# A Transformer layer on one core: the Newton steps of its small reciprocal roots move from VectorE to GpSimd

## What is computed

```
h = x @ w_in                                  # split into q, k, v, z, beta, a (delta rule), q, k, v (attention), two gates
o_a = gated_deltanet(...)                     # conv of 4 taps, silu, l2-norm of q and k, delta rule in chunks of 64
o_b = diff_attention(...)                     # two softmaxes per head, p0 - lam * p1, times v, then RMS norm per head
merged = sigmoid(ga) * (o_a @ w_branch_a) + sigmoid(gb) * (o_b @ w_branch_b)
x = layer_norm(ALPHA * x + merged @ w_out)
ffn = (silu(x @ w_gate) * (x @ w_up)) @ w_down
x = layer_norm(ALPHA * x + ffn)

l2_normalize(x) = x * rsqrt(sum(x * x) + 1e-6)
rms_norm(x, w)  = x * rsqrt(mean(x * x) + 1e-6) * w
```

## Time and profile before

| | |
|---|---|
| median of 3 runs | 2053.83 us (2053.8 to 2054.26) |
| the profiled execution's own time | 2053.67 us |
| its span in the profile | 2051.9 us |
| PE busy | 2003.6 us, 98% |
| DVE busy | 1234.3 us, 60% |
| ACT busy | 915.8 us, 45% |
| POOL busy | 0.2 us, 4 instructions |

### The profile page before, as it was taken

The page is one execution under the profiler, slowest core; times in us unless marked ns, Lnnn a source line. Parts: engine busy times, 40 slices in busy tenths (PEclk is TensorE's granted clock), DMA queues, the critical chain, the costliest instruction groups (busy, mean ns, idle before and its releaser), DMA issues.

```text
span 2051.9 us, 32409 instructions
## 1 busy us (share of the span) xinstructions
PE 2003.6 (98%) x11050; PEld 1649.2 (80%) x11050; DVE 1234.3 (60%) x1750; ACT 915.8 (45%) x1194; POOL 0.2 (0%) x4
## 2 busy tenths in 40 slices
PE   9999999999999999999999999799999999999996
PEld 6887888878887878787888887588888888888884
DVE  7768767587646666767655555644554444554455
ACT  5435344353445555555534433444443444443442
POOL 0000000000000000000000000000000000000000
PEclk9999999999999999999999999999999999999998
DMA  7434343343454545454555676365555555555553
GB/s 252 131 128 134 119 144 131 125 143 114 156 190 158 179 159 183 155 176 163 187 191 190 199 241 214 107 190 190 188 187 195 191 192 190 190 190 192 189 192 140
DMA packets 97961, 353.14 MB, mean 172 GB/s; under 512 B 10816, under 2 KB 11072, under 8 KB 97728
## 3 DMA queue, kind: packets, MB, share of 16 engines
q1 hardware_dynamic: 97856, 351.64, 52.2%
HBM read 349.50 MB, written 2.10 MB: 171 GB/s over the span
## 4 chain that ended last, share of the span: by engine, by line
PE 89%; DVE 5%; ACT 2%; issue 2%; DMA 0%; SPq 0%; DVEq 0%; ACTq 0%
PE pg L337 80%; PE B L337 7%; DVE wlo L989 1%; DVE gates L989 1%; ACT whi L708 1%; PE B L610 1%; DVE cT L997 0%; DMA vn<-in_xT 0%; PE B L410 0%; DVE od L989 0%; PE B L565 0%; DVE pr L997 0%; PE B L586 0%; ACT pr L888 0%; ACT L774 0%
## 5 line engine op out<-in xcount | busy, mean ns | idle before, releaser
L989 DVE TENSOR_TENSOR wlo<-raw,whi 128x1024 fp32r<-128x1024 f32 (+1 forms) x650 | 791.3, 1221 | 626.0 <-ACT whi L708 614.2
L708 ACT ACTIVATE whi<-raw 128x1024 fp32r<-128x1024 f32 (+1 forms) x650 | 684.4, 1057 | 702.3 <-PE pg L337 695.2
L337 PE MATMUL pg<-whi,act_x 128*128 128x512 f32 x3008 | 980.0, 397 | 0.0
L337 PEld LDWEIGHTS pg<-whi,act_x 128*128 128x128 f32 x3008 | 565.1, 188 | 122.6 <-issue 5.5
L337 PE MATMUL pg<-wlo,act_x 128*128 128x512 f32 x1504 | 586.7, 390 | 0.0
L337 PE MATMUL pg<-whi,act_a 128*128 128x512 f32 x1664 | 519.6, 391 | 5.5 <-DVE act_a L989 5.5
L337 PEld LDWEIGHTS pg<-whi,act_a 128*128 128x128 f32 x1664 | 313.2, 188 | 71.7 <-DVE act_a L989 7.2
L337 PEld LDWEIGHTS pg<-wlo,act_x 128*128 128x128 f32 x1504 | 283.1, 188 | 54.4 <-issue 1.2
L337 PE MATMUL pg<-wlo,act_a 128*128 128x512 f32 x832 | 324.7, 390 | 0.0
L337 PEld LDWEIGHTS pg<-wlo,act_a 128*128 128x128 f32 x832 | 156.7, 188 | 31.9
L337 PE MATMUL pg<-whi,act_b 128*128 128x512 f32 x512 | 158.8, 390 | 0.0
(11 more groups left out here) (183 smaller groups left out, 983.8 us busy)
## 6 DMA issues: line engine op xcount, KB each, us to landing
raw<-in_weights SPq DMA_DIRECT2D x646, 512.0 KB, 3.8
gates<-in_ln_in SPq DMA_DIRECT2D x4, 512.0 KB, 6.5
gates<-in_ln_in SPq DMA_DIRECT2D x1, 2048.0 KB, 9.6
out<-gates SPq DMA_DIRECT2D x8, 256.0 KB, 2.5
raw<-in_weights SPq DMA_DIRECT2D x4, 256.0 KB, 4.3
cT<-in_xT SPq DMA_DIRECT2D x2, 512.0 KB, 7.1
qT<-in_xrow SPq DMA_DIRECT2D x2, 512.0 KB, 7.1
kT<-in_xrow SPq DMA_DIRECT2D x2, 512.0 KB, 5.2
```

The source lines that it names most:

```text
L337: return nc.tensor.matmul(o, l, r, start=start, stop=stop)
L708: return nc.scalar.activation(o, i, ACT.Copy, scale=scale)
L989: return V.tensor_tensor(o, a, b, op)
```

## The change

The three Newton steps of `rk`, `rs` and the heads' root go to a program of GpSimd's own (`@block.gpsimd`). DVE keeps the seed, now in one operation (the bits times -0.5 plus the constant) instead of two, and hands it over by a semaphore (`dve_ss`, `dve_qs`, `dve_oss`). GpSimd does four operations per Newton step, 12 per root, each one waiting for the one before it, and hands back by `pool_rinv`, `pool_rs`, `pool_oss`. DVE's `oh` moves from slot s0 + 5 to slot s0 + 6. The layer norms keep `rsqrt` on DVE, with the one-operation seed.

```diff
--- before.py
+++ after.py
@@ -37,7 +37,7 @@
 DA_TURN = [(21, 23), (27, 29)]
 DA_TURN_FIRST = [(10, 12), (18, 20)]
 HEAD_SLOTS = [0, 6, 12, 18]
-CONV_LINKS, BUILD_LINKS, SCAN_LINKS, DA_LINKS = 12, 22, 18, 69
+CONV_LINKS, BUILD_LINKS, SCAN_LINKS, DA_LINKS = 12, 10, 7, 25
 OT_SLOTS = (12, 14)
 XP = [(0, 2), (2, 4), (4, 8), (8, 12), (12, 16)]
 HALVED = 2
@@ -133,6 +133,7 @@
         cw = sb("cw", [P, 3, HB, CONV])
         sm = sb("sm", [P, 72])
         dsm = sb("dsm", [P, NDS])
+        half = sb("half", [P, 8])
         lam = sb("lam", [P, 2])
         g_all = sb("g_all", [P, TOK * HEADS])
         pz = sb("pz", [P, 4, TOK * HEADS])
@@ -219,7 +220,7 @@
             pe_z dve_vn pe_so act_s act_o0 pe_ks dve_r pe_o1 dve_o1 pe_qtok act_osq act_sqq
             dve_oh pe_oT act_oT dve_oT
             pe_qkT act_qkT pe_s dve_s1 dve_mx act_exp dve_pd pe_pT act_pT pe_pv act_oss dve_oh2 pe_oT2
-            act_oT2 dve_oT2 dve_m pe_mT act_mT dve_mT conv_chain build_chain scan_chain da_chain""".split()
+            act_oT2 dve_oT2 dve_m pe_mT act_mT dve_mT dve_qs pool_rs dve_ss pool_rinv dve_oss pool_oss pool_chain conv_chain build_chain scan_chain da_chain""".split()
         N = {n: sem(n) for n in once + counted}
 
         class Chain:
@@ -981,6 +982,36 @@
                 normalize(1, cq)
 
 
+        @block.gpsimd
+        def _(pool):
+            G = nc.gpsimd
+            ch = Chain(pool, N["pool_chain"], 1)
+
+            def root(o, x):
+
+                a = half[:, 0:x.shape[1]]
+                for i in range(3):
+                    ch(G.tensor_tensor(a, o, o, ALU.mult))
+                    ch(G.tensor_tensor(a, a, x, ALU.mult))
+                    ch(G.tensor_scalar(a, a, -0.5, 1.5, ALU.mult, ALU.add))
+                    last = G.tensor_tensor(o, a, o, ALU.mult)
+                    if i < 2:
+                        ch(last)
+                return last
+
+            for j in range(NB + 1):
+                if j > 0:
+                    pool.wait_ge(N["dve_qs"], 1 + j)
+                    root(d_("rs"), d_("qs")).then_inc(N["pool_rs"], 1)
+                if j < NB:
+                    pool.wait_ge(N["dve_ss"], 1 + j + 1)
+                    ch(root(d_("rk"), d_("ss")))
+                    G.tensor_tensor(d_("rinv"), d_("rk"), d_("ss"), ALU.mult).then_inc(N["pool_rinv"], 1)
+            for h in range(HEADS):
+                pool.wait_ge(N["dve_oss"], 1 + h + 1)
+                root(sm[:, 48:50], sm[:, 42:44]).then_inc(N["pool_oss"], 1)
+
+
         @block.vector
         def _(dve):
             V = nc.vector
@@ -996,11 +1027,14 @@
             def stt(o, a, s, b, op0, op1):
                 return V.scalar_tensor_tensor(out=o, in0=a, scalar=s, in1=b, op0=op0, op1=op1)
 
+            def seed(o, x):
+
+                return ts(o.bitcast(I32), x.bitcast(I32), -0.5, ALU.mult, float(0x5F3759DF), ALU.add)
+
             def rsqrt(ch, o, x):
 
                 a = sm[:, 64:64 + x.shape[1]]
-                ch(V.tensor_single_scalar(o.bitcast(I32), x.bitcast(I32), 1, ALU.logical_shift_right))
-                ch(ts(o.bitcast(I32), o.bitcast(I32), -1.0, ALU.mult, float(0x5F3759DF), ALU.add))
+                ch(seed(o, x))
                 for _ in range(3):
                     ch(stt(a, o, -0.5, o, ALU.mult, ALU.mult))
                     ch(tt(a, a, x, ALU.mult))
@@ -1121,6 +1155,7 @@
                     ch(ts(d_("ss"), d_("ss"), RMS_EPS, ALU.add))
                     ch(V.reciprocal(d_("e"), d_("ss")))
                     ch(tt(d_("e"), d_("e"), s_("beta"), ALU.mult))
+                    seed(d_("rk"), d_("ss")).then_inc(N["dve_ss"], 1)
                 if s == 14:
                     dve.wait_ge(N["act_decay"], 1 + j + 1)
                     ch(tt(AT[:, :, :], decm[:, :, :], bc(d_("e"), P), ALU.mult))
@@ -1155,14 +1190,13 @@
                             tt(T[0:CH], T[0:CH], B8[3][0:CH], ALU.subtract)
                             tt(TTf[0:CH, :, 0:CH], TT[0:CH], B8[2][0:CH], ALU.subtract)
                             tt(TTf[CH:P, :, CH:P], TT[CH:P], B8[2][CH:P], ALU.subtract).then_inc(N["dve_t"], 1)
-                if s == 19:
-                    rsqrt(ch, d_("rk"), d_("ss"))
-                    ch(tt(d_("rinv"), d_("rk"), d_("ss"), ALU.mult))
                 if s == 25:
                     ch(tt(decm[:, :, :], decm[:, :, :], rep(c("same"), 8), ALU.mult))
                 if s in (20, 22):
                     t = (s - 20) // 2
                     dve.wait_ge(N["pe_v"], 1 + 2 * j + t + 1)
+                    if t == 0:
+                        dve.wait_ge(N["pool_rinv"], 1 + j + 1)
                     tt(vr[:, t], B4[0], bc(d_("rinv")[:, HB * t:HB * (t + 1)], P), ALU.mult).then_inc(N["dve_v"], 1)
                 if s in (28, 29):
                     t = s - 28
@@ -1196,9 +1230,9 @@
                     ch(V.tensor_reduce(d_("qs"), AT[:, :, :], X, ALU.add))
                     ch(ts(d_("qs"), d_("qs"), P * RMS_EPS, ALU.mult, P * RMS_EPS ** 2, ALU.add))
                     ch(stt(d_("qs"), d_("os"), 1.0 / P, d_("qs"), ALU.mult, ALU.add))
-                if s == 7:
-                    rsqrt(ch, d_("rs"), d_("qs"))
+                    seed(d_("rs"), d_("qs")).then_inc(N["dve_qs"], 1)
                 if s == 10:
+                    dve.wait_ge(N["pool_rs"], 1 + j + 1)
                     for t in range(TOK):
                         tt(od[:, t], od[:, t], bc(d_("rs")[:, HB * t:HB * (t + 1)], P), ALU.mult
                            ).then_inc(N["dve_oh"], 1)
@@ -1258,9 +1292,11 @@
                         ins.then_inc(N["dve_pd"], 1)
                     if s == s0 + 5:
                         dve.wait_ge(N["act_oss"], 1 + HB * j + h + 1)
+                        ch(ts(sm[:, 42:44], sm[:, 40:42], 1.0 / P, ALU.mult, RMS_EPS, ALU.add))
+                        seed(sm[:, 48:50], sm[:, 42:44]).then_inc(N["dve_oss"], 1)
+                    if s == s0 + 6:
+                        dve.wait_ge(N["pool_oss"], 1 + HB * j + h + 1)
                         dve.wait_ge(N["pe_oT2"], 1 + HB * j + h)
-                        ch(ts(sm[:, 42:44], sm[:, 40:42], 1.0 / P, ALU.mult, RMS_EPS, ALU.add))
-                        rsqrt(ch, sm[:, 48:50], sm[:, 42:44])
                         ch(tt(oh[:, :, :], B[3][:, 0:SEQ].rearrange("p (t d) -> p t d", t=TOK), bc(sm[:, 48:50], P),
                               ALU.mult))
                         stt(oh[:, :, :], oh[:, :, :], 1.0 - LAMBDA_INIT, rep(par[:, slice(*PARAM["daw"])], TOK),
```

## The result

| | before | changed |
|---|---|---|
| median, us | 2054.02 (8 runs, 2053.58 to 2054.9) | 2060.37 (8 runs, 2056.86 to 2061.15) |
| profiled execution, us | 2053.67 | 2060.26 |
| its span, us | 2051.9 | 2058.2 |

By the medians the changed kernel is slower by 6.3 us, where 16 were forecast. The ratio is 1.0027, with a 95% interval of 1.0016 to 1.0038, or 5.6 us; that is what the means give (2059.7 and 2054.1), which lie closer together than the medians. The direction was right and the time lies in the range, but the size was off by 10 us: two terms of the sum were mis-sized and a third was missing. The changed kernel's eight runs spread over 4.3 us, where the eight of before spread over 1.3 (in larger groups of 20 to 23 runs, those of before spread over 2.4 to 2.7).

The account below looks back on a forecast made before the run. PE, busy 98% of the span, was taken as the bound. Gains of -2.0 us and +18.0 us for the heads made +16.0 us on 2053.83, say 2070 us; forecast's own range 2058 to 2092, 8-in-10 range 2054 to 2105.

Parts of the forecast that it names:

- T: Attention heads: time of the root on GpSimd with handovers and one standstill, forecast as 5.07 us.
- a link at 0.32 us: GpSimd's root: each of 12 chained operations takes 0.32 us, the geometric middle of 0.20 and 0.50.
- The hold of a whole `wlo`: Heads' root: a GpSimd operation beside DVE's wide `wlo` stands still for its whole 1.13 us.
- the heads' term: Attention bodies: later `oh` and scores make PE wait 4.50 us per body, +18.0 us in four.
- the delta rule's -1.6 us: Delta rule: without the small operations `wlo` and the convolution start 0.54 us earlier, in three bodies -1.6 us.
- the gains: Delta rule's three bodies -1.6 us and both layer norms -0.4 us, together -2.0 us.
- So its wait stays as it is in PE's time: Delta rule: ACT's work up to the decay hangs on the convolution, so PE's three 0.8 us waits remain.
- the root was thus free: Attention head 0: DVE's root only filled time in which DVE would have waited for ACT's `whi` anyway.
- a fall of PE's clock: New PE waits: a fall there would prove the forecast wrong; none seen beside waits of 1 us.
- quick or side by side: Rival: GpSimd is quick or works beside `wlo`, T at most 4.23 us, within 0.2% (4.1 us); chance 0.28.
- Faster: Rival: `oh` ahead of the scores costs nothing and T fits, -2.0 us, 2051.8 us; chance 0.04.
- A slow link: Rival: a GpSimd link of 0.50 us, T = 7.23 us, sum 2109 us; slower than forecast had chance 0.18.

Follow-up runs that it names:

- e4: Changed kernel with two Newton steps instead of three for the heads' root, 8 links instead of 12 and less exact; 2050.06 us.
- e7: Changed kernel with DVE's wait for the root, `oh` and scores ahead of `wlo` at slots 6, 12, 18 and 24; 2049.34 us.
- e1: Changed kernel with the heads' root back on DVE at slot s0 + 5, only the delta rule's two roots on GpSimd; 2048.32 us.
- e10: e3 with the delta rule's `rs` root at slot 9 instead of 7, still on DVE; 2052.89 us.
- e5: Changed kernel with two unused 128x384 matmuls on PE at each body's head 1, ahead of its wait for `pr`; 2055.8 us.
- e3: Kernel before with only the one-operation seed, nothing on GpSimd; 2053.4 us.
- e8: Changed kernel with `oh` left in slot s0 + 5, so that DVE stands still for GpSimd's root; 2058.62 us.
- e9: e3 with the next head's scores ahead of the slot's `wlo` at slots 6, 12 and 18, nothing on GpSimd; 2049.84 us.
- e6: e1 with the next head's scores ahead of the slot's `wlo` at slots 6, 12 and 18; 2043.98 us.
- e2: Changed kernel with the delta rule's roots back on DVE, only the heads' root on GpSimd; 2065.23 us.

## Why the prediction was wrong in size

**The mechanism held.** Forecast were a lower wait at the convolution, waits for `oh`, a longer wait for `pr`, one held link in each head, and the scores of head 1 later by T - 3.13 us. T, from the seed's end to the return, is 740.04 - 735.65 = 4.39 us. The formula gives 1.26 us for the scores, and 5.56 - 4.30 = 1.26 were measured; it gives no wait for `oh` at heads 0 to 2, none seen (16 waits had been forecast, and there are four); 0.58 at head 3, and 0.36 to 0.80 were seen; for `pr` 2.25, measured 2.17. Per body it makes 0.58 + 1.26 = 1.84 us, and 101.6 to 101.7 less 99.77 are 1.8 to 1.9. The 0.80 us at the very last head has another cause than the root: `oh` stands there behind a `wlo` that waits until 1002.40 us for ACT's `whi`, and 0.62 us of it stay in e4, whose root is four links shorter.

**The first failed step: a link at 0.32 us, and so T = 5.07.** Measured is 0.28 us (0.20 of work and 0.08 to the next). The hold of a whole `wlo` was rightly taken; it measured 1.02 us, 1.22 less the operation's own 0.20, against the 1.13 of the sum. T was 0.68 us too long, 0.59 of it in the links and 0.11 in the hold. At T = 4.39 the root is back for `oh` in time at heads 0 to 2, so that a body loses the 1.84 us above and not 4.50, and the heads' term is +7.4 us and not +18.0. The middle between "as on DVE" and "as ACT on 256 columns" should have leaned to the lower bound: it was the row with the same operation and the same few columns, and the memset of 0.10 us had already shown that GpSimd starts an operation quickly.

The Trainium skill's page GPSIMD Engine Reference, section Performance versus the Vector engine, gives the factor 1.96 for an elementwise operation with two inputs, measured at N = 2048. This trace differs for so small an operation: 0.20 us on GpSimd (e7: 193 to 197 ns) against 161 ns on DVE is a factor of 1.2. No run here has a wide operation on GpSimd, so the page's own case is neither borne out nor refuted.

**The second failed step: "the second starts at 298.37 right behind them, though its `whi` was ready at 297.80", the delta rule's -1.6 us.** I paired that `wlo` with the `whi` that was nearest in time. It used the one before it, which ended at 294.89, as the changed kernel shows: there two `wlo` run in a row with no wait for ACT. Timeline of ACT before:

```profile
293.83 1.06 ACT L708 ACTIVATE whi<-raw 128x1024 fp32r<-128x1024 f32 x1
```

So not 0.54 us came off DVE's path to the convolution but the whole root, over 2 us, and with it both of PE's waits, for the convolution and for the decay, 2.7 + 2.5 = 5.2 us. With 0.7 us less waiting for `pr` and 0.2 at the layer norm through the one-operation seed, that is about what e1 gains, 6.0 us; the gains were forecast as 2.0. "So its wait stays as it is in PE's time", said of the decay, fell with it: the decay's wait hangs on all that DVE has to do up to it, as e10 shows, where the convolution is in time and the decay still waits 1.05 us. The same pairing error stands in "the root was thus free" for the heads; there it did not change the sum, since the path from the small chain to the scores was counted from its rows.

**The third: no term for the clock.** The text named a fall of PE's clock as what would make it wrong, and judged by the waits of 1 us, which show none. At 2.17 us it does fall, in two of the four bodies of the profiled execution, 1.6 us each, and e5 puts its price at 4.6 us on the median. The trace of before had a warning: "at the full clock in all but the last slices" was read from digits that stand for 90% or more. The long wait of 8.32 us at the first layer norm, which ends at 1289.10 us, has PE at half its clock from about 1286 to 1296 us (granted clock in a window, before):

```profile
1286.00:1296.00 10.00, 5.34 (x15) 3.92 (x16) 7.45 (x13) 6.48 (x9) 0.00 (x0) 0.50 0.05 9
```

So a forecast wait of 2.3 us lay between waits without a fall (up to 1.41 us, the kernel's first few microseconds left aside) and one with a fall.

**The sum as measured.** -6.0 (e1) + 7.5 (e1 to e5) + 4.6 (e5 to the changed kernel) = +6.1 us. These are steps from one kernel to the next, so that they must add up to the measured 6.3 but for noise. The checks that could have failed are each step's own: 6.3 us by place for the delta rule, 4 x 1.84 = 7.4 for the heads, and 2 x 1.6 = 3.2 for the two falls of the profiled execution. Against the forecast, the heads cost 10.5 us less and the gains are 4.0 larger, and the missing 4.6 us of clock hid a part of both errors. Without the clock the kernel would have stood at 2055.8 (e5), outside the forecast's own range of 2058 to 2092: that the time lies in it is luck.

The rivals: "quick or side by side" had the right side in the link but not in the hold; its bound of T = 4.23 was missed by 0.16 us, and without the clock the changed kernel would have been within it (e5, +1.5 us). "Faster" was given to nothing but a free `oh`; e1 shows that a gain of 6 us lay in the change, hidden by what the heads cost. "A slow link" fell.

One difference between traces has nothing to do with the change. The profiled changed kernel is 6.0 us ahead of before at its first attention body, less its longer wait, and e1 is only 5.2 ahead (its transposes stand at 648.12). But the executions already differ at 40 us, where PE's wait for `lam` ends (timelines of PE: before, changed, e1):

```profile
39.88 0.63 PE L337 MATMUL B<-g_all,cst 128*128 128x32 f32 x4 [0.84 <-DVE lam L994]
40.17 0.63 PE L338 MATMUL B<-g_all,cst 128*128 128x32 f32 x4 [0.84 <-DVE lam L1025]
40.94 0.63 PE L338 MATMUL B<-g_all,cst 128*128 128x32 f32 x4 [0.85 <-DVE lam L1022]
```

Counted from there, both gain 6.3 us.

What stays open: why the clock falls behind one wait of 2.17 us and not behind the next was not found. The last 1.1 us of the profiled span come from the stretch behind the first layer norm, in which the clock returned about 3.4 us later in the changed kernel than in before; it did so in e3, e5, e7, e8, e9 and e10 too and not in e1, e2, e4 and e6, which goes with no edit.

## What to carry to other kernels

When an operation may have waited for one of several like transfers or tiles, find its partner by the semaphore's count in the program, or by whether it waits once the work ahead is gone, and not by what ends nearest in time. Move to a slower engine the small chains that have slots to spare, and leave those in a chain that ends in TensorE's wait; where a chain must stay, look at what stands ahead of it for no reason (here one `wlo`, 4 us). A wait of TensorE that grows past the longest one behind which the trace shows no fall of its clock needs a term, or at least a rival with a price, for that clock; look for falls in narrow windows, since slices of 50 us hide them.

## What the runs showed of the hardware

- A GpSimd operation on 128x2 or 128x8 takes 0.20 us, and a chain of them with a semaphore between any two starts one each 0.28 us.
- GpSimd stands still beside a DVE operation that reads two inputs from SBUF: of its 296 operations in the changed kernel 47 last over 0.25 us, up to 1.22, and every one of them overlaps such an operation (mostly `wlo`), while each short one that lies wholly within a wide DVE operation has one there that takes an input from PSUM. In e7 and e8, where no `wlo` meets a head's root, 31 are left. In the delta rule (timeline of POOL in the changed kernel) two are held by the two `wlo` from 293.12 to 295.48, nine in a row run at 0.20 us beside the convolution, which reads PSUM and a single large input of SBUF, and the last is held by the `wlo` of 298.00:

```profile
293.20 1.20 POOL L994 TENSOR_TENSOR half<-dsm 128x8 f32<-128x8 f32 x1 [97.61 <-DVE dsm L1025]
294.48 1.06 POOL L995 TENSOR_TENSOR half<-half,dsm 128x8 f32<-128x8 f32 x1
295.63 0.20 POOL L996 TENSOR_SCALAR half<-half 128x8 f32<-128x8 f32 x1
...
297.90 0.20 POOL L996 TENSOR_SCALAR half<-half 128x8 f32<-128x8 f32 x1
298.18 1.10 POOL L997 TENSOR_TENSOR dsm<-half,dsm 128x8 f32<-128x8 f32 x1
```

- The Trainium skill's page SBUF — State Buffer, section Who interferes with whom, states that a VectorE instruction with two inputs in SBUF contends with a GpSimd instruction that reads SBUF, and that one with at most one, outside the modes that use both ports, does not. The trace agrees, for GpSimd's side of it. That DVE is held up in turn these rows don't show: `wlo` takes 1.23 us with and without GpSimd.
- TensorE's granted clock fell to its half level (1.2 GHz) at five of twelve waits of 2.14 to 2.27 us (two each in the changed kernel and e8, one in e2), at a price of about 1.6 us each. It fell at the wait of 8.1 to 8.3 us of the first layer norm in every kernel, and at none of the waits for `pr` of 1.15 us or less (e1, e4, e5, e7). That the changed kernel's runs spread so wide because they differ in how often it fell is not shown run by run, since each kernel has one trace; their mean granted clocks, 0.990 to 0.993 in the order of their times, speak for it.
